# First two input groups of the last block taken from unnormalised tokens: root and shift column applied where the products are drained

## The reference

```python
# end of the first model
h = h + conv_ffn(rms_norm(h, ffn_norm[1]), w_up[1], conv_w[1], conv_b[1], w_down[1])
x = rms_norm(h, final_norm)[:, N_META:]
# start of the second model
mod = c_act @ w_ada + b_ada                       # six vectors: sh1, sc1, ga1, sh2, sc2, ga2
h   = rmsnorm(x, ln1_pre) * (1.0 + sc1) + sh1
proj = h @ w_in                                   # 2816 columns: q_a, k_a, v_a, q_h, f_h, i_h, g_h
```

## Time and profile before

| what | value |
|---|---|
| median of 3 runs | 1121.56 us (1120.48 to 1122.22) |
| profiled execution, on the device | 1120.37 us |
| its span from first to last instruction | 1118.6 us |
| TensorE matmuls busy | 1086.9 us, 97% |
| DVE busy | 685.1 us, 61% |
| ACT busy | 521.0 us, 47% |
| mean granted TensorE clock | 0.993 |

### The profile page before, as it was taken

One profiled execution on the slowest core, in us unless ns is written; L12 is line 12 of the kernel. 1 busy time (PEld: TensorE's weight loads), 2 busy tenths in 40 slices (PEclk: granted clock), 3 DMA queues, 4 the chain that ended last, 5 costly groups with the idle time before them and its releaser, 6 DMA issues.

```text
span 1118.6 us, 20870 instructions
## 1 busy us (share of the span) xinstructions
PE 1086.9 (97%) x8533; PEld 939.4 (84%) x8533; DVE 685.1 (61%) x1280; ACT 521.0 (47%) x900; POOL 100.9 (9%) x161
## 2 busy tenths in 40 slices
PE   7999999999999999999999999899999999999996
PEld 5899899999999888999999999798999655555453
DVE  5685798888845566598889854777546631111114
ACT  4544666565543454476556644574454221111113
POOL 5010000000000000010004000000100022222210
PEclk9999999999999999999999999899999999999998
DMA  9564476777556545376777556454348599999993
GB/s 276 191 230 157 152 226 176 202 225 215 184 172 186 157 143 180 125 240 176 211 222 207 174 175 190 103 188 119 100 158 341 190 407 418 416 417 415 416 412 144
DMA packets 201504, 252.70 MB, mean 226 GB/s; under 512 B 21828, under 2 KB 181105, under 8 KB 189121
## 3 DMA queue, kind: packets, MB, share of 16 engines
q1 hardware_dynamic: 187406, 223.65, 59.1%
q0 software_dynamic: 13584, 27.55, 7.2%
q10 hardware_dynamic: 419, 0.16, 0.1%
HBM read 273.34 MB, written 11.53 MB: 255 GB/s over the span
## 4 chain that ended last, share of the span: by engine, by line
PE 80%; DVE 8%; ACT 5%; DMA 4%; issue 2%; SPq 0%; DVEq 0%; ACTq 0%
PE ps L881 17%; PE ps L882 17%; PE ps L883 16%; PE ps L2827 10%; PE ps L2840 5%; DVE wlo L848 2%; DMA over_wlo<-in_w_exp_gate 2%; ACT whi L828 2%; DMA we<-in_w_exp_gate 2%; PE ps L787 2%; PE ps L2410 1%; PE ps L971 1%; PE ps L2801 1%; PE ps L2540 1%; PE ps L2385 1%
## 5 line engine op out<-in xcount | busy, mean ns | idle before, releaser
L881 PE MATMUL ps<-xhi,whi 128*128 128x272 f32 (+2 forms) x1392 | 410.7, 295 | 5.8 <-DVE xlo L1926 3.0
L882 PE MATMUL ps<-xlo,whi 128*128 128x272 f32 (+2 forms) x1392 | 400.0, 287 | 0.0
L883 PE MATMUL ps<-xhi,wlo 128*128 128x272 f32 (+2 forms) x1392 | 398.8, 286 | 0.0
L848 DVE TENSOR_TENSOR wlo<-raw,whi 128x2048 fp32r<-128x2048 f32 (+1 forms) x112 | 252.4, 2255 | 115.6 <-ACT whi L828 115.4
L828 ACT ACTIVATE whi<-raw 128x2048 fp32r<-128x2048 f32 (+1 forms) x112 | 210.9, 1883 | 157.9 <-PE ps L883 157.4
L881 PEld LDWEIGHTS ps<-xhi,whi 128*128 128x128 f32 x1392 | 263.9, 190 | 13.1 <-issue 9.4
L882 PEld LDWEIGHTS ps<-xlo,whi 128*128 128x128 f32 x1392 | 263.8, 190 | 1.2 <-issue 0.5
L883 PEld LDWEIGHTS ps<-xhi,wlo 128*128 128x128 f32 x1392 | 263.5, 189 | 0.0
L881 PE MATMUL ps<-hhi,whi 128*128 128x272 f32 (+2 forms) x384 | 111.0, 289 | 1.3 <-DVE wlo L848 0.9
L882 PE MATMUL ps<-hlo,whi 128*128 128x272 f32 (+2 forms) x384 | 109.3, 285 | 0.0
L883 PE MATMUL ps<-hhi,wlo 128*128 128x272 f32 (+2 forms) x384 | 109.0, 284 | 0.0
(11 more groups left out here) (477 smaller groups left out, 1675.2 us busy)
## 6 DMA issues: line engine op xcount, KB each, us to landing
raw<-in_w_up SPq DMA_DIRECT2D x88, 512.0 KB
raw<-in_w_in SPq DMA_DIRECT2D x32, 1024.0 KB
ada<-in_w_ada POOLq DMA_DIRECT2D x48, 512.0 KB, 5.1
raw<-in_w_down SPq DMA_DIRECT2D x16, 896.0 KB
raw<-in_w_exp_up SPq DMA_DIRECT2D x11, 1024.0 KB
raw<-in_w_exp_gate SPq DMA_DIRECT2D x10, 1024.0 KB
raw<-in_w_exp_down SPq DMA_DIRECT2D x10, 1024.0 KB
raw<-in_w_out SPq DMA_DIRECT2D x8, 1024.0 KB
```

The source lines that it names most:

```text
L848: dve.tensor_tensor(wlo[SLOT[n]][:, 0:nk, :], raw[n % RAW][:, 0:nk, :], whi[SLOT[n]][:, 0:nk, :].bitcast(F32), ALU.subtract).then_inc(s_w_ ...
L881: pe.matmul(dst, ah, bh, start=first, stop=False, **kw)
L882: pe.matmul(dst, ah, bl, start=False, stop=False, **kw)
L883: return pe.matmul(dst, al, bh, start=False, stop=last, **kw)
```

## The change

1. `mod_columns(5)` moves from behind the averages to ahead of the first down group. What DVE makes of the adaptive vectors (`conditioning`) moves from behind the averages to ahead of the residuals of the last layer's down groups, and gets two small steps: the first shift vector, as hi and lo, is put in two extra columns of two new tiles, `raw3_hi` and `raw3_lo`, [128, 8, 258].
2. In the down groups ACT makes `raw3_hi` = XT * `both_gains` per tile (two a group, behind the squares) and DVE `raw3_lo` (two a group, ahead of the next residual; tiles 6 and 7 behind the split of the second chunk).
3. The first two groups of the block (ka, qa 0) multiply their weights with `raw3`, 258 columns wide, half a group to a bank. The averages of both statistics are put between the tiles of the first.
4. For these two groups DVE multiplies the products by the root (`root_drain`), after it has taken the shift's column, and ACT adds the column (and for qa 0 the factor 0.125).
5. `modulated` makes tiles 0 to 3 of XN, then drains ka, splits the third chunk, makes the rest for the nine other groups, then drains qa 0. ACT's split of the second chunk moves ahead of the last squares, that of the third ahead of the root.
6. TensorE too waits for POOL's last constants ahead of the first scores, as DVE does; `epst` becomes a column of `bc44`; 128 bytes of SBUF are left free, so that `raw3` fits over the buffers of `w_ada`.

```diff
+        raw3_hi, raw3_lo = (sb(n, [P, KT, T2 + 2], F32R, at=m) for n in ("raw3_hi", "raw3_lo"))
...
+        def raw_third_hi(act, k):
+            act.wait_ge(s_gsc.sem, s_gsc.after())
+            act.activation(raw3_hi[:, k, 0:T2], XT[:, k, META:T], ACT.Copy, scale=both_gains[:, k:k + 1]).then_inc(s_x_hi.sem, s_x_hi.event(("raw third",), k))
+
+        def raw_third_lo(dve, k):
+            dve.wait_ge(s_gsc.sem, s_gsc.after("column lo"))
+            dve.wait_ge(s_x_hi.sem, s_x_hi.after(("raw third",), k))
+            dve.scalar_tensor_tensor(raw3_lo[:, k, 0:T2], XT[:, k, META:T], both_gains[:, k:k + 1], raw3_hi[:, k, 0:T2].bitcast(F32), ALU.mult, ALU.subtract).then_inc(s_x_lo.sem, s_x_lo.event(("raw third",), k))
...
+                raw_third = g[0] == "in2" and g[2] < 2
+                fresh = xkey is not None and g[2] == {"n2": 1, "n3": 2}.get(xkey[0], 0)
...
+                            if raw_third:
+                                mm = product(pe, ps[b + mt][:, 0:T2 + 2], h[:, k, c], lo[:, k, c], raw3_hi[:, k, :],
+                                             raw3_lo[:, k, :], at == 0, at == nk - 1)
...
-                    split_hi(act, CHUNK_NO[(g, 2)] + 1)
+                    split_hi(act, CHUNK_NO[(g, 2)] + (2 if g == ("down", DEPTH - 1, 3) else 1))
...
+                    if l == DEPTH - 1:
+                        for t in range(2):
+                            raw_third_hi(act, 2 * i + t)
+
+            split_hi(act, SECOND_AT + 2)
...
-            shifted_hi(act, ("n3",), 0)
+            shifted_hi(act, ("n3",), 0, range(4))
+            act.wait_ge(s_drained_dve.sem, s_drained_dve.after(("in2", 0, 0)))
+            drain(("in2", 0, 0), kaT[:, :], kaT[:, :], ACT.Identity, bias=column[:, 0:1], last=False)
+            drain(("in2", 0, 0), vaT[:, :], vaT[:, :], ACT.Identity, bias=column[:, 1:2])
+            shifted_hi(act, ("n3",), 0, range(4, KT))
...
+                if i == 1:
+                    act.wait_ge(s_drained_dve.sem, s_drained_dve.after(g))
+                    for t in range(2):
+                        drain(g, qaT[:, t, :], qaT[:, t, :], ACT.Identity, scale=0.125, bias=column[:, 2 + t:3 + t], last=t == 1)
+                elif name == "ka":
+                    pass
...
+            def conditioning():
+
+                dve.wait_ge(s_ada_used.sem, s_ada_used.after(5))
+                dve.tensor_tensor(mod[:, :], ps[7][:, 0:48], col("b_ada", 0, 48), ALU.add).then_inc(s_mod.sem, s_mod.event())
+                dve.wait_ge(s_mod.sem, s_mod.after())
...
+                dve.wait_ge(s_gsc.sem, s_gsc.after("scales"))
+                dve.tensor_tensor(both_gains[:, :], gsc[:, 0, :], col("final_norm", 0, KT), ALU.mult).then_inc(s_gsc.sem, s_gsc.event())
...
+                shifts = mod[:, 0:KT].rearrange("p (k o) -> p k o", o=1).broadcast_to([P, KT, 2])
+                dve.tensor_copy(raw3_hi[:, :, T2:T2 + 2], shifts).then_inc(s_gsc.sem, s_gsc.event("column hi"))
+                dve.wait_ge(s_gsc.sem, s_gsc.after("column hi"))
+                dve.tensor_tensor(raw3_lo[:, :, T2:T2 + 2], shifts, raw3_hi[:, :, T2:T2 + 2].bitcast(F32), ALU.subtract).then_inc(s_gsc.sem, s_gsc.event("column lo"))
+
...
+                        if kind == "down" and l == DEPTH - 1 and j >= 0:
+                            raw_third_lo(dve, j)
...
+                if l == DEPTH - 1:
+                    conditioning()
...
+            split_lo(dve, SECOND_AT + 1)
+            for k in (6, 7):
+                raw_third_lo(dve, k)
...
+            def root_drain(i, dst, scale):
+
+                g = ("in2", 0, i)
+                product_done(dve, g)
+                for t in range(2):
+                    dve.tensor_scalar(column[:, 2 * i + t:2 * i + t + 1], ps[pair(g) + t][:, T2:T2 + 1], scale, None, ALU.mult)
+                for t in range(2):
+                    o = dve.tensor_tensor(dst[t], ps[pair(g) + t][:, 0:T2], RS(("n3",)), ALU.mult)
+                o.then_inc(s_drained_dve.sem, s_drained_dve.event(g))
...
+                def scaled(k):
+                    dve.scalar_tensor_tensor(XN[:, k, 0:T2], XT[:, k, META:T], both_gains[:, k:k + 1], RS(key), ALU.mult, ALU.mult).then_inc(s_scaled_n.sem, s_scaled_n.event(key, k))
+
+                for k in range(4):
+                    scaled(k)
+                root_drain(0, (kaT[:, :], vaT[:, :]), 1.0)
+                split_lo(dve, SECOND_AT + 2)
+                for k in range(KT):
+                    if k < 4:
+                        scaled(k + 4)
+                    dve.wait_ge(s_x_hi.sem, s_x_hi.after(key, k))
+                    dve.scalar_tensor_tensor(xlo[:, k, 0:T2], XN[:, k, 0:T2], mod[:, sh + k:sh + k + 1], xhi[:, k, 0:T2].bitcast(F32), ALU.add, ALU.subtract).then_inc(s_x_lo.sem, s_x_lo.event(key, k))
+                root_drain(1, (qaT[:, 0, :], qaT[:, 1, :]), 0.125)
...
-                key = ("n1", l + 1) if l + 1 < DEPTH else ("nf",)
+                if l == DEPTH - 1:
+                    mod_columns(pe, 3 * l + 2)
                 for i in range(4):
                     gemm(pe, ("down", l, i), None, T, c0=DOWN_FROM[l])
-                if l == DEPTH - 1:
-                    for i in (5, 6, 7):
-                        stat_average(pe, key, i)
-                        stat_average(pe, ("n3",), i)
-                    pe.wait_ge(s_logged.sem, s_logged.after(key))
-                    pe.wait_ge(s_root_sq.sem, s_root_sq.after())
-                    mod_columns(pe, 3 * l + 2)
...
+                if m == 0:
+                    pe.wait_ge(s_consts.sem, s_consts.after("second"))
...
+                if i == 0 and k in (0, 3, 4):
+                    for key in (("nf",), ("n3",)):
+                        stat_average(pe, key, {0: 5, 3: 6, 4: 7}[k])
...
-                gemm(pe, ("in2", 0, i), ("n3",), T2, tokens=name == "ih", between=within2)
+                gemm(pe, ("in2", 0, i), ("n3",) if i >= 2 else ("raw third",), T2, tokens=name == "ih", between=within2)
```

More of the change, by code:

```diff
@@ L248, in build @@
         ada = [sb(f"ada{i}", [P, D]) for i in range(ADA)]
+        sb("column_room", [P, 32])
+        m = [ada_at, ada_at + 2 * 4 * KT * (T2 + 2)]
+        raw3_hi, raw3_lo = (sb(n, [P, KT, T2 + 2], F32R, at=m) for n in ("raw3_hi", "raw3_lo"))
         m = [ada_at, ada_at + 2 * 8 * CW * 4]
@@ L291, in build @@
         rows44 = sb("rows44", [1, 44])
-        bc44 = sb("bc44", [P, 44])
-        epst = sb("epst", [P, 1])
+        bc44 = sb("bc44", [P, 45])
+        epst = bc44[:, 44:45]
         mod = sb("mod", [P, 48])
@@ L331, in build @@
         P2, PT2 = sb("P2", [P, 2, 384], at=m), sb("PT2", [P, 2, 384], at=m)
+        column = sb("column", [P, 4], at=m)
         m = [first_at, early_end]
@@ L587, in root_read @@
                 eng.wait_ge(s_xt.sem, s_xt.after("f", KT - 1))
-            elif kind in ("n3", "n5"):
+            elif kind == "n3":
+                eng.wait_ge(s_drained_dve.sem, s_drained_dve.after(("in2", 0, 1)))
+            elif kind == "n5":
                 eng.wait_ge(s_scaled_n.sem, s_scaled_n.after(key, KT - 1))
@@ L853, in x_hi, with shifted_hi @@
             act.activation(xhi[:, k, 0:w], src, ACT.Copy).then_inc(s_x_hi.sem, s_x_hi.event(key, k))
-        def shifted_hi(act, key, sh):
-            for k in range(KT):
+        def shifted_hi(act, key, sh, ks):
+            for k in ks:
                 act.wait_ge(s_scaled_n.sem, s_scaled_n.after(key, k))
@@ L901, in gemm @@
                 k0 = DOWN_K[j][0] if g[0] == "down" else RAW_UP if raw_up else 0
-                fresh = xkey is not None and g[2] == (1 if xkey[0] == "n2" else 0)
+                raw_third = g[0] == "in2" and g[2] < 2
+                fresh = xkey is not None and g[2] == {"n2": 1, "n3": 2}.get(xkey[0], 0)
                 if g[0] == "down" and g[2] == 0:
@@ L1451, in _ @@
                 product_done(act, g)
-                if name == "ka":
-                    drain(g, kaT[:, :], ps[b][:, 0:T2], last=False)
-                    drain(g, vaT[:, :], ps[b][:, T2:2 * T2])
+                if i == 1:
[4 more added lines that the diff above has]
+                    pass
                 elif name == "qa":
```

34 lines of the change are left out of this document (11 added, 23 removed).

## The result

| | before | changed |
|---|---|---|
| median, 17 runs each, same chip | 1121.32 us (1119.84 to 1122.82) | 1124.78 us (1122.10 to 1127.86) |
| ratio, 95% interval | | 1.0031 (1.0022 to 1.0040) |
| profiled execution, on the device | 1120.37 us | 1123.02 us |
| its span | 1118.6 us | 1121.0 us |
| its mean granted clock | 0.993 | 0.998 |

The change makes the kernel 3.5 us slower. Two more series, each beside the kernel before on its own chip, gave ratios of 1.0044 (1.0029 to 1.0060) and 1.0054 (1.0040 to 1.0068). The profiled execution is 2.65 us longer than that of before, less than the medians differ. All readings from here to the experiments are of this one execution.

A forecast was written before the change was run, and what follows sets the result against it. TensorE was the bound, busy 97%, held by ACT's and DVE's chains in down groups and DVE's list in the block. 1.7 + 4.0 - 2.4 = +3.3 on 1120.37, plus 1.2 to the median: 1124.8 us, range 1120.8 to 1127.8.

The forecast's parts named there:

- rival (c): In the new waits: the clock falls in one or two, adding 1.7 to 3.4 us, about 1127.3 us; chance 0.14.
- Columns: Ahead of the down groups: the moved turn costs 1.95 us, less a covered 0.26 us wait, +1.7 us.
- Copies and rests: In the down groups: two copies and two rests each delay the next group's second chunk, 0.8 + 1.6 + 1.6 = +4.0 us.
- D: Point where the next matmul could follow the last down matmul, 703.37 before; later times count from each kernel's own.
- Rival (b): In the down groups: they hide the copies, so 1.7 - 2.4 = -0.7, 1120.9 us; chance 0.11.
- Transition: Down groups to first maximum: TensorE seems to gain 8.6 us, but DVE's list leaves -2.4 us.
- two single columns: In the drain of ka on DVE: two one-column instructions of unknown price, taken as 0.1, between nothing and 0.3 us.
- (a): In the block: DVE does not hold it, transition gives -6.0 us, 1121.3 us; chance 0.11.
- (d): Down groups and block: neither copies nor DVE's list cost, or fh 0 is quicker, 1117.5 us; chance 0.09.
- Sum: Whole kernel: 1.7 + 4.0 - 2.4 = +3.3 us, with bounds +1.6 to +4.8 us.
- The clock: In the new waits: no fall taken in the sum; a 4 us fall would cost up to 1.7 us.

The follow-up runs named there:

- copies_in_pauses: Changed kernel with ACT's copies and DVE's rests of tiles 0 to 5 moved behind the chunk work TensorE waits for in the down groups; 1120.15 us, ratio 0.9991.
- finals_behind: Changed kernel with the eight final-norm scalings moved from ahead of the first maxima to group 7, behind the first probabilities; 1122.83 us, ratio 1.0025.
- qa_ahead: Changed kernel with the drain of qa 0 moved forward, on DVE behind the fourth rest, on ACT ahead of the fourth chunk's rounding; 1126.38 us, ratio 1.0044.
- changed_third: Changed kernel unaltered, run a third time, beside the kernel before on its own chip; 1126.83 us, ratio 1.0054.
- waits_filled_less: Changed kernel with 11 unread matmuls ahead of the first scores and 9 ahead of the first probabilities; 1127.82 us, ratio 1.0054.
- changed_again: Changed kernel unaltered, run a second time, beside the kernel before on its own chip; 1125.89 us, ratio 1.0044.
- copies_finals: Changed kernel with copies and rests moved behind the down groups' chunk work and the final scalings behind the first probabilities; 1119.51 us, ratio 0.9986.
- all_moved: Changed kernel with copies, rests, final scalings and down groups' sums of squares moved later, and the drain of qa 0 moved ahead; 1116.50 us, ratio 0.9962.

## Why the prediction was right

The forecast was 1124.8 us and 0.59 for slower; the median is 1124.78 us. The agreement is closer than the argument deserves: the profiled execution grew by 2.65 us and not by 3.3, and falls of the clock, which the sum left out, made up for it in most of the others. That these two miss each other by so little is luck. Only a part of the falls is rival (c), to which I gave 0.14.

**Columns.** Forecast +1.7, measured +1.22 us (640.45 less 639.23). I had taken the modelled duration of the turn. From its start to the next start is 1.70 us, and it covers what stood there before: 0.48 us from 638.75 to 639.23. DVE's vectors lay in DVE's wait, as forecast: they run from 650.50 to 651.98, and 1.42 us of idle time are left ahead of the next rest.

**Copies and rests.** Forecast +4.0; D moved by 5.05 us, less 1.22 makes 3.83. The waits are 0.86, 1.53 and 2.23 us for 1, 1.8 and 2.4. Against the kernel before, the distance between the starts of the two matmuls around each wait grows by 0.82, 1.49 and 1.63 us, forecast 0.8, 1.6 and 1.6. They grow because DVE's rests, 0.40 us each, stand ahead of the residual from group 1 on. Rival (b) is out: the down groups hid nothing; copies_in_pauses shows that they could have.

**Transition.** Forecast -2.4; the first maximum starts at D+27.2 (forecast 27.7, before 30.1), so -2.9 us. The two single columns cost 0.13 us from start to the drain behind them (0.1 taken). qa 0 is drained at D+19.6 (19.7). The scores wait 2.70 us (2.6) and the probabilities 2.25 (2.8), both for the engine named. The bound is DVE's list: finals_behind takes 3.3 us out of it and the trace is 3.0 us shorter, while qa_ahead only reorders it and gains nothing. Rivals (a) and (d) are out for the changed kernel, but (d)'s 1117.5 us is about what the mended ones reach.

**Sum.** 1.22 + 3.83 - 2.9 = +2.1 us, which is the 2.13 us of the keys' turn. At the first expert matmul it is 1.63 us (878.01 against 876.38), since the kernel before has a stretch of half rate from 857 to 860 and this execution none. At the end it is 2.4 us in the span, 0.8 of it from the experts' stretch, which is open.

**The clock.** The sum took no fall. In 19 of 26 executions of the changed kernel the mean clock is below 0.995; these have medians of 1125.09 and 1126.83 us, the seven others 1123.12. For the kernel before the three classes lie within 1.4 us. So a part of the median, 1.7 to 3.7 us by series, goes with the clock. The traces price the falls one by one. *In the down groups:* behind the wait ahead of group 3's second chunk a fall puts D 1.5 us later, counted from the start of the columns (71.22 us in changed_third and 71.18 in waits_filled_less for 69.67). My estimate was up to 1.7. *At the scores:* behind the wait of 2.70 us it costs nothing up to the keys' turn, in changed_again and in changed_third, because the wait ahead of the probabilities takes it up. So rival (c) prices this one wrongly. *At the router:* from the keys' turn to the first expert matmul it takes 116.7 us where the clock does not fall, 117.2 us with a fall of some 3.5 us (as in the kernel before) and 118.8 us with one of 7 us (changed_third, copies_in_pauses). No rival had this one. From the columns to the end changed_third is 4.5 us longer than the first execution: 1.55 us from the down groups, 2.1 from the router, 0.8 from the experts' stretch.

How much a long wait costs by the clock is shown for copies_finals, which has no wait ahead of the probabilities to take a fall up: filling its one long wait takes the median from 1119.51 to 1116.17 us (two chips, ratios 0.9986 and 0.9953, intervals apart). all_moved, whose longest wait is 1.40 us, fits: it reaches 1116.50 us with no clock below 0.994, though its trace is no shorter than that of copies_finals. In the changed kernel itself the filled waits shortened nothing, and whether the router's fall depends on what came before it is open.

The Trainium skill (TensorE: Matmul & The Clock Gate, Part 1: The HAM clock gate) has the throttled state as the default, released by activity, and says that the number of slow matmuls at a kernel's start differs from run to run of one kernel. The traces agree: at the start of the program matmuls of 272 columns start 0.22 to 0.23 us apart and then 0.12 to 0.13, and the step lies at 17.2, 17.5 and 16.6 us in three executions of the changed kernel. The later falls differ likewise: changed_again and changed_third fall behind the wait of 2.70 us and the first execution doesn't. My reason for weighing it low, that rows of before showed no single wait followed by the half rate, was no evidence: they held no such wait in dense work.

## What to carry to other kernels

When work is added to an engine that prepares operands, its place in the queue matters more than its length: the same copies cost 3.8 us ahead of a chunk's rounding and nothing behind it. A gap closed on TensorE is worth only what the preparing engine's own list allows, so follow that list to its last customer; reordering it moves the wait, and only what leaves it shortens the time. And where executions of one kernel differ in mean clock, find each fall in a trace and price it by the distance between two points that all executions share, before taking a difference of medians for a difference of schedules. An equal mean clock does not make two kernels comparable: a fall ahead of another wait cost nothing here, one behind a wait of 2.2 us in dense work cost 1.5 us more, and one far behind the change up to 2.1 us.

## What the runs showed of the hardware

- Behind waits of 2.20 to 2.70 us in dense work the granted clock fell to 0.50 in some executions and stayed at 1.00 in others of the same program. In the wait of 4.58 us of qa_ahead it fell before the wait was over. Behind the waits of 0.86 and 1.53 us in the down groups, and of 1.05 and 1.40 us in all_moved, no profile here shows a fall.
- Falls without a wait occur too: 857 to 860 in the kernel before, behind 32 matmuls of 36 columns in the router (from 853.36), and 781 to 784 in waits_filled_less. In the profiled executions the fall at the router lasts some 3.5 us in four, 7 us in two, and is absent from the others. What it goes with is open.
- A fall costs only what no later wait takes up: 0.01 us in changed_again up to the keys' turn, 1.5 us behind the down groups' wait.
- Unread matmuls are no loss where TensorE would stand still, but their price must be read first: one 128x128 matmul in fp32 is two records of 0.112 us, not one of 0.134 as the count in a grouped row had made me take.
